# Attention outputs that leave the values transposed with weights applied before, and a last expert whose rows are added by a product

## The reference

```python
# layer 1, per head; p_c, p_s, p_w are softmax weights of the three branches
return gb[:, :, 0] * o_c + gb[:, :, 1] * o_s + gb[:, :, 2] * o_w
...
def expert_block(args):
    xblk, e = args
    hid = jax.nn.silu(xblk @ w_gate[e]) * (xblk @ w_up[e])
    return hid @ w_down[e]
...
y = jnp.zeros_like(xt).at[row_token].add(yb * row_weight[:, None].astype(yb.dtype))
```

## Time and profile before

| what | us |
|---|---|
| median of 3 runs | 1696.51 (1694.89 to 1697.32) |
| the profiled execution | 1696.19 |
| its span | 1694.4 |
| attention of layer 0 | 203 to 254 |
| experts of layer 0, first product to last | 330 to 802 |
| attention of layer 1 | 1001 to 1122 |
| experts of layer 1, first product to last | 1196 to 1670 |

### The profile page before, as it was taken

How to read it: one execution, slowest core, us unless ns; L and a number is a source line. 1 busy time by engine, 2 the same in 40 slices (tenths; PEclk the granted TensorE clock), 3 DMA queues, 4 the chain that set the end, 5 groups by cost and what they waited for, 6 DMA issues and landing times.

```text
span 1694.4 us, 20980 instructions
## 1 busy us (share of the span) xinstructions
PE 1589.3 (94%) x7948; PEld 753.0 (44%) x7948; DVE 434.3 (26%) x1112; ACT 393.7 (23%) x897; POOL 200.4 (12%) x297
## 2 busy tenths in 40 slices
PE   7999899799999999998799989999799999999993
PEld 4545574433333333332446457855333333333331
DVE  1585651610000000000321235643500000000002
ACT  2444451311111111111100136632211111111110
POOL 1241220000000000000101012320000000000000
PEclk9999999899999999999899989999799999999997
DMA  7120307379999999999924120042699999999996
GB/s 236 64 86 7 112 5 297 137 300 421 421 422 421 422 421 423 422 422 371 302 34 170 39 66 2 1 184 115 250 413 422 421 421 422 422 422 422 423 422 248
DMA packets 117162, 467.24 MB, mean 276 GB/s; under 512 B 40346, under 2 KB 46746, under 8 KB 68205
## 3 DMA queue, kind: packets, MB, share of 16 engines
q1 hardware_dynamic: 107724, 449.63, 66.1%
q10 hardware_dynamic: 4256, 8.40, 1.4%
q0 software_dynamic: 5120, 8.41, 1.3%
HBM read 455.88 MB, written 18.91 MB: 280 GB/s over the span
## 4 chain that ended last, share of the span: by engine, by line
PE 77%; SPq 11%; DMA 5%; DVE 3%; issue 2%; ACT 1%; POOL 1%; ACTq 0%; DVEq 0%; POOLq 0%
PE bank L1793 19%; PE bank L1806 10%; SPq L1741 9%; PE bank L1768 9%; PE bank L1432 8%; PE bank L558 7%; PE bank L811 6%; PE bank L446 4%; DMA arena<-in_moe_w_up 3%; PE bank L411 3%; PE bank L1783 2%; SPq L1750 2%; PE bank L892 2%; PE bank L428 2%; PE bank L1799 1%
## 5 line engine op out<-in xcount | busy, mean ns | idle before, releaser
L1793 PE MATMUL bank<-arena 128*64 128x512 f32 x2048 | 451.4, 592 | 8.1 <-DMA arena<-in_moe_w_up 6.7
L1793 PEld LDWEIGHTS bank<-arena 128*64 128x64 f32 x2048 | 143.5, 137 | 304.6 <-issue 294.0
L1806 PE MATMUL bank<-arena 128*64 128x512 f32 x1024 | 230.6, 592 | 2.2 <-DVE arena L1897 2.2
L1893 DVE TENSOR_TENSOR arena<-arena,bank 128x256 f32<-128x256 f32 x64 | 26.9, 421 | 644.4 <-ACT arena L1883 644.4
L1768 PE MATMUL bank<-arena 128*64 128x512 bf16 x1280 | 168.2, 395 | 9.7 <-DVE arena L1763 6.4
L1812 POOL DMA_INDIRECT y_d<-arena,slot_row x64 | 62.7, 979 | 904.7 <-ACT arena L1888 891.1
L1432 PE MATMUL bank<-arena 128*128 128x512 f32 x320 | 138.1, 593 | 0.8 <-ACT arena L328 0.8
L1806 PEld LDWEIGHTS bank<-arena 128*64 128x64 f32 x1024 | 72.2, 137 | 124.5 <-issue 111.2
L1883 ACT ACTIVATE arena<-bank 128x256 f32<-128x256 f32 x64 | 24.5, 383 | 408.2 <-PE bank L1793 408.2
L558 PE MATMUL bank<-arena 128*128 128x512 f32 x256 | 111.9, 594 | 0.0
L811 PE MATMUL bank<-arena 128*128 128x512 f32 (+1 forms) x288 | 105.3, 525 | 0.0
(11 more groups left out here) (287 smaller groups left out, 1434.8 us busy)
## 6 DMA issues: line engine op xcount, KB each, us to landing
arena<-in_moe_w_gate SPq DMA_DIRECT2D x128, 1024.0 KB, 20.1
arena<-in_moe_w_up SPq DMA_DIRECT2D x128, 1024.0 KB, 22.9
arena<-in_moe_w_down SPq DMA_DIRECT2D x62, 2048.0 KB, 23.2
arena<-in_even_w_in SPq DMA_DIRECT2D x4, 2048.0 KB, 7.9
arena<-y_d ACTq DMA_DIRECT2D x8, 1024.0 KB, 8.2
arena<-bias_row_d SPq DMA_DIRECT2D x2, 3584.0 KB, 11.6
arena<-in_odd_w_in SPq DMA_DIRECT2D x3, 2048.0 KB, 8.9
arena<-in_even_w_out SPq DMA_DIRECT2D x2, 2048.0 KB, 8.0
```

What stands on the lines that cost most here:

```text
L1793: mm = nc.tensor.matmul(bank[1][fh * CAP:(fh + 1) * CAP, :], xeT[:, j, half * CAP:(half + 1) * CAP], wgu[u][:, :, n, fh * FH:(fh + 1) * FH ...
L1806: mm = nc.tensor.matmul(bank[3][dh * CAP:(dh + 1) * CAP, :], hidT[:, j, fh * CAP:(fh + 1) * CAP], wd[u][:, n, dh * 512:(dh + 1) * 512], st ...
```

## The change

**Attention.** Units are put together into quads: four heads of one tile and one branch. Layer 1's quads come as selected, window, compressed for each group of four heads; layer 0's as heads 0 to 3 and 4 to 7. When the four exponentials are there, GpSimd makes the four weights (1/sum, with the gate in layer 1), and VectorE multiplies the exponentials by them before they are transposed, 1024 columns at a time at 512 keys, 768 at 384 and a whole quad from 256 down. Transposes stand six steps behind their unit, so values at least seven behind the quad's last one. In the values product the operands trade places: the values are loaded, the transposed weights of four heads are the moving operand (512 columns in layer 1, two products of 256 columns onto the two halves of the output partitions in layer 0). The output comes out transposed as the projection needs it; layer 1's three branches and all their key tiles are summed in one bank. ScalarE copies it once per four heads. `even_finish`, `odd_finish` and the twelve turns of attention output are gone; four turns of the Mamba half stay. The copies out of the transposes' banks alternate between ScalarE and VectorE. Eight slots hold exponentials instead of four. The first product of the projection is done before the last quad's transposes.

**Last expert.** Expert 31 isn't scattered. VectorE makes ones times weights for its slots (`last_ones`), TensorE transposes them (`last_T`), and two products per tile with the expert's 64 rows per half go into eight banks; VectorE adds them. Rows of the other 31 experts are fetched by SP as soon as expert 30 has been scattered, into weight slot 0, and are added with weights that are 0 where the expert is the last. Because rows of the last expert are never written, `y_d` is filled with zeros first, from a zeroed `z`, by two DMAs of 4 MB that ScalarE issues in the even mixer; `z` is written only when they are done. Two chunks of layer 1's projection weights are loaded behind the fetch instead of one ahead of it, and a third after the last products.

```diff
             def pe(self, pe, drain):
+                for t in range(self.steps):
+                    if t < len(self.units):
+                        u = self.units[t]
+                        if not (u.get("paired") and u["r"] % 2):
+                            self.scores(pe, [u, self.units[t + 1]] if u.get("paired") else [u])
+                    if t == len(self.units) + NT:
+                        drain()
+                    for g in self.turn_at[t]:
+                        self.turn(pe, g)
+                    for q, kt in self.value_at[t]:
+                        self.values(pe, q, kt)
...
+            TURN, SCALE = 6, 2
...
+                    L, last = q["L"], 4 * n + 3
...
+                    per = 4 if 4 * L <= DM else 2
+                    for k in range(4 // per):
+                        c["s"] += 1
+                        for u in q["units"][per * k:per * k + per]:
+                            u["scaled"] = c["s"]
+                        self.scale_at[last + self.SCALE + k].append(dict(quad=q, lo=per * k, n=per))
+                    q["scaled"] = c["s"]
+                    per, q["groups"] = NT // q["nk"], []
+                    for lo in range(0, 4, per):
...
+                        self.turn_at[4 * n + lo + per - 1 + self.TURN].append(g)
+                    for kt in range(q["nk"]):
+                        self.value_at[last + self.TURN + 1 + kt].append((q, kt))
+                    q["o"] = c["o"]
+                    if q["last"]:
+                        self.out_at[last + self.TURN + 1 + q["nk"]].append(q)
...
             def act(self, act):
+                for t in range(self.steps):
+                    for g in self.turn_at[t]:
+                        if g["copy"] == "act":
+                            self.copy_out(act, g)
+                    for q in self.out_at[t]:
+                        act.wait_ge(self.sem("pv"), q["m"] + 1)
+                        nc.scalar.activation(q["dst"], split(bank[4 + q["o"] % 2][:, :], 4, P), ACT.Copy).then_inc(self.sem("o"), 1)
...
             def dve(self, dve, link):
...
                         dve.wait_ge(self.sem("qk"), u["a"] + 1)
-                        if u["a"] - 4 >= self.base["a"]:
-                            dve.wait_ge(self.sem("tr"), self.by_a[u["a"] - 4]["n"] + 1)
+                        if t >= 8:
+                            dve.wait_ge(self.sem("tr"), self.units[t - 8]["group"]["n"] + 1)
...
+                    for op in self.scale_at[t]:
+                        q, lo, n = op["quad"], op["lo"], op["n"]
+                        slot = q["units"][lo]["a"] % 8
+                        p = self.p[:, slot:slot + n, 0:q["L"]]
+                        dve.wait_ge(self.sem("coef"), q["m"] + 1)
+                        nc.vector.tensor_tensor(p, p, att_coef[:, q["m"] % 4, lo:lo + n].unsqueeze(2).broadcast_to((P, n, q["L"])),
+                                                ALU.mult).then_inc(self.sem("sc"), 1)
+                    for g in self.turn_at[t]:
+                        if g["copy"] == "dve":
+                            self.copy_out(dve, g)
...
                 if c == 0:
+                    act.wait_ge(S("zeros"), past("zeros") + 1)
+                    for q in range(2):
+                        act.dma_start(y_d[q].rearrange("(p a r) c -> p a (r c)", p=P, a=4),
+                                      z.rearrange("p i c -> p (i c)").unsqueeze(1).broadcast_to((P, 4, NT * DI))).then_inc(S("y_zero"), 16)
...
+            act.wait_ge(S("y_zero"), past("y_zero") + 32)
             for i in range(NT):
                 n = J_Z + i
                 ev(n, z[:, i, :], bank[n % 4][:, :]).then_inc(S("ep_ev"), 1)
...
+            sp.wait_ge(S(f"{t}_gu"), L * NE + NE - 1)
+            fence(sp, t, L)
+            fetch(lambda i: f"{t}_yin{i}")
             if L == 0:
                 odd_early(sp)
...
+            pe.wait_ge(S("m_lT"), past("m_lT") + L + 1)
+            pe.wait_ge(S(f"{t}_y"), L * NE + NE + 1)
+            for i in range(NT):
+                for h in range(2):
+                    cs = slice(h * CAP, (h + 1) * CAP)
+                    mm = nc.tensor.matmul(bank[2 * i + h][:, :], last_T[cs, i * P:(i + 1) * P], yb[cs, (NE - 1) % RING, :],
+                                          start=True, stop=True)
+                mm.then_inc(S("m_fin"), 1)
...
+            add_fetched(0)
+            for i in range(1, NT):
+                add_fetched(i)
+                add_last(i - 1)
+            add_last(NT - 1)
```

More of the change, by code:

```diff
@@ L398, in done @@
             def done(self, eng):
-                self.finished(eng, len(self.order) - 1)
+                self.out(eng, self.after["o"] - 1)
             def mixed(self, eng, i):
-                for u in self.all:
-                    if "src" in u and u["tile"] == i:
-                        self.copied(eng, u)
+                for g in self.groups:
+                    if g.get("tile") == i:
+                        self.copied(eng, g)
+                self.out(eng, max(q["o"] for q in self.quads if q["tile"] == i))
             def scores(self, pe, us):
@@ L450, in pe @@
-            def pe(self, pe):
-                N = len(self.seq)
-                for t in range(N + 3):
-                    u = self.seq[t] if t < N else {}
-                    if "m" in u and not (u.get("paired") and u["b"] % 2):
-                        self.scores(pe, [u, self.seq[t + 1]] if u.get("paired") else [u])
-                    if 2 <= t < N + 2:
-                        self.turn(pe, self.seq[t - 2])
-                    if t >= 3 and "m" in self.seq[t - 3]:
-                        self.values(pe, self.seq[t - 3])
@@ L586, in route, with drain @@
                     mm.then_inc(S("m_rmm"), 1)
-            project(0, TILES[0])
-            att.tail_turns(pe)
-            for i in TILES[1:]:
+            def drain():
+                att.scored(pe, att.after["a"] - 1)
+                project(0, TILES[0])
+            att.pe(pe, drain)
+            project(0, TILES[1])
+            att.done(pe)
+            for i in TILES[2:]:
                 project(0, i)
@@ new lines, in products, with even_turn @@
+            def products(o, pT, kt):
+                return [(o[r * HD:(r + 1) * HD, half * 2 * P:(half + 1) * 2 * P], kvd[:, kt, O_V:O_V + HD], pT[:, r::2, :])
+                        for r in range(2)]
+            return dict(tile=i, L=L, units=units, products=products, first=half == 0, fresh=True, ends=True, last=half == 1,
+                        dst=mixT[:, 4:8, i * P:(i + 1) * P])
+        def even_turn(i):
+            return dict(tile=i, src=rows_m[:, 0, i, :], dst=mixT[:, 0:4, i * P:(i + 1) * P], ready=(S("ssm_row"), NT))
@@ L1350, in build @@
+        even_att = Attention([even_quad(i, half) for i in TILES for half in range(2)],
+                             {1 + i: even_turn(i) for i in range(NT)}, 2 * EW + 2 * KD * 512, O_XBCS, even_weigh)
         o0 = HEADS * TW
@@ L1689, in build @@
+        odd_att = Attention([odd_quad(i, g, b) for i in TILES for g in range(OG) for b in (SEL, WIN, CMP)],
+                            {}, O_OW + 2 * KD * 512, O_CT, odd_weigh, before=even_att)
         weight = sb("weight", [P, 2, NT])
@@ L2045, in body @@
                 down(pe, t, c, cu, u)
+                if after == 1:
+                    pe.wait_ge(S("m_lones"), past("m_lones") + L + 1)
+                    for i in range(NT):
+                        mm = nc.tensor.transpose(bank[7][:, i * P:(i + 1) * P], last_w[:, i].rearrange("p h s -> p (h s)"), ident[:])
+                    mm.then_inc(S("m_lturn"), 1)
             per_expert(pe, L, body)
```

367 lines of the change are left out of this document (187 added, 180 removed).

## The result

The changed kernel takes 1728.7 us, median of four runs (1722.3 to 1731.1), against 1696.9 (1694.9 to 1699.6) for the kernel before beside it: 1.018 times as long, 95% interval 1.0147 to 1.0214. I had forecast 1698.6 and a range up to 1708. The profiled execution is the shortest of the four, 1722.3, with a span of 1720.4, so 26.0 more than the span before.

| stretch | before | after | change |
|---|---|---|---|
| layer 0: first logits to projection | 48.0 | 45.3 | -2.7 |
| layer 0: projection and router | 76.2 | 77.9 | +1.7 |
| layer 0: copy of the last expert's y to the square of the next norm's tile 3 | 21.9 | 15.1 | -6.8 |
| layer 1: first logits to projection | 119.0 | 159.3 | +40.3 |
| layer 1: projection and router | 74.2 | 76.1 | +1.9 |

What follows compares the result with a forecast made beforehand. TensorE, busy 94% of the span, was taken as the bound, with latency chains after the last expert. 1696.2 - 6.3 - 7.3 - 3 + 19 = 1698.6 us; own range 1693 to 1704, with rivals 1685 to 1708.

Steps and rivals of the forecast that it cites:

- Tails: After the last expert in both layers: earlier fetch and last rows by products gain 6.3 and 7.3 us, together 13.6.
- Layer 0's attention: Output turns removed and values in two column halves: net -3 us, bounds -8 and +4.
- A gain of 8, as by the speedup alone: Layer 0's values by the skill's table, up to 2x at 64 columns: 8 us instead of 3, sum 1693.6.
- Layer 1's attention: TensorE waits for quads' weights and slots: 121.7 to about 140.5 us, net +19, bounds +8 and +24.
- rival B: Granted clock falls in layer 1's attention stalls, slow products follow: +8 us, 1706.6; chance 0.18.
- the clock leaves 1.00 there: Sign in layer 1's long tiles that the forecast is wrong in size; gaps above 5 us were the other.
- The other two quads' weights are covered: Layer 1's long tiles: besides window's weights and the slot reuse, the selected and compressed quads' weights cost no stall.
- stalls in the long tiles: Layer 1, per twelve units: about 3.3 us before window's transpose and 1.2 for slot reuse at 512 keys; similar at 384.
- Edits taken as nothing: Zeroing y_d, ScalarE's new wait, later MoE weight loads and GpSimd's last wait cost nothing; zeroing uncovered up to 2 us.
- A: Faster: in layer 1 only the window stall remains (+10), layer 0's column halves cost no drain (-6): 1686.6; chance 0.28.
- C: Tails' fetch ends no earlier: gain 7 instead of 13.6 us, 1705.2; chance 0.12 shared with D.
- D: Two halves of layer 0's values don't overlap: +4 us instead of -3, 1705.6; chance 0.12 shared with C.

Runs made afterwards that it cites:

- run 4: Changed kernel plus filler products where TensorE stands still in layer 1's attention, into a transposes' bank that is overwritten afterwards; 1717.9 us.
- run 3: Changed kernel with layer 1's weights made on VectorE just ahead of the quad's scaling, none on GpSimd; 1721.6 us.
- run 2: Changed kernel with one swap in VectorE's order: the copy of a transposed block stands ahead of the next quad's scaling; 1710.7 us.
- run 5: Changed kernel with copies ahead of scalings, and twelve slots instead of eight for layer 1's exponentials; 1705.7 us.
- run 6: Changed kernel with copies ahead of scalings, twelve slots, and layer 1's transposes eight steps behind their unit instead of six; 1691.0 us.
- run 1: Kernel before, with its old attention, given only the new ends of both layers and the zeroing of y_d; 1683.5 us, ratio 0.9914.

## Why the prediction was right or wrong, step by step

**Tails: right.** Forecast 6.3 and 7.3, in the profiles 6.8 and 7.4, alone on the chip 13.5 against 13.6. The intermediate steps held too: fetch issued at 793.7 (forecast 794.8), first additions at 799.7 (800.5), the last additions of tile 3 from 812.7 to 815.2 (816.7, in a run that was 1.0 earlier). By my own terms the sums come to 800.1 for the first landing and to gains of 6.4 and 7.5, a few tenths that change nothing.

**Layer 0's attention: right at its cut, a third of it in the whole layer.** Forecast -3, measured -2.7. But the end of the stage moved: the last quad's transposes and values now stand behind the projection's first product. From first logits to the experts' first product it is 124.2 before and 123.2 after, so 1.0 remains. The stage also varies with the clock: the same code took 45.3 in after, 45.6 in run 4 and 47.5 in run 3. And TensorE was 87% busy in it, not over 90% as I had said. The price of the change between half and full array holds in the timeline of after: values and transposes in turn start 0.58 and 0.59 apart.

```profile
220.75 0.65 PE L471 MATMUL bank<-arena 128*64 128x256 f32 x4
221.33 0.66 PE L456 MATMUL bank<-ident,arena 128*128 128x128 f32 x4
221.92 0.44 PE L471 MATMUL bank<-arena 128*64 128x256 f32 x2
```

One such pair, four value records and four transposes, takes 1.17. I had 0.78 + 0.44 = 1.22. A gain of 8, as by the speedup alone, did not come.

**Layer 1's attention: wrong by half, +19 forecast, +40 measured.** From first logits to projection that is 140.4 against 159.3. Of the 18.9 between them 14.4 are the clock, 3.6 idle time and 0.9 work. Another 2.7 is my starting point: I took 121.7 for the old attention, which from its first logits to the projection takes 119.0.

The step that failed first is the choice between the forecast and rival B. I had put the clock's fall at 18 in 100 and at 8 us, because the clock had stayed 1.00 at 83% busy in the last tile. But there the idle time came in pieces of 0.7 at most, here in pieces of up to 4.3, so that tile told little of this stage. The recorded sign "the clock leaves 1.00 there" came true: the term was wrong in size, and what was left out of it is the clock's 14.4. The size of a piece doesn't decide alone either, as the last section shows. Run 4 moves the clock's cost while the waits stay, and the time follows; run 2 moves both.

The step that failed second is "The other two quads' weights are covered". I had asked who needs the scaling's result, and found the transposes. I had not asked what stands behind the scaling in VectorE's own queue: the copy of the quad before it, behind that this quad's values, and behind the values on TensorE the last scores of the quad after next. So the weights and values of neighbouring quads were strung into one chain. The copies alternate between ScalarE and VectorE, and at 128 keys TensorE's idle time before the values is 2.0, 2.4 and 3.0 where VectorE copies and 0.6 to 1.3 where ScalarE does. At 256 keys my idle time was 6.8 against 10.2, and with the swap it is 7.2. At 128 keys my 10.4 looks right beside 11.1, but for a wrong reason: I had a round over the weights that ends at the transposes, the idle time lies before the values, and a third of it left with one swap. In the profiles the swap takes 11.4 off the attention, 6.1 idle time, 4.9 clock and 0.4 work. The rest of the 18 by the medians lies in executions without a trace; their granted clocks, below, point to the clock again.

What I had worked out as stalls in the long tiles was right: 9.0 and 8.8 against 8.9 and 8.4, the large piece 3.45 against 3.3, the small one 1.0 against 1.2, and in runs 5 and 6 they went away for the most part. At 512 keys the sum agrees partly by luck: it holds 2.14 before the very first transposes, which I had not listed, and in the first round window's piece was only 2.32.

**Edits taken as nothing.** The zeroing: right, by run 1. That the first product hides the last quad's transposes and values: only their latency. They moved behind it with their work, and the projection is 1.9 longer, which I had not counted. The 1.7 more in layer 0's projection I had not forecast at all. In run 1, with the old attention, it is the clock: 0.84 in the first 11 us of the projection, where it was 1.00 before. In after it is the last quad's work and 0.8 of idle time before its values.

**The rivals.** A (only the window stall remains, column halves cost nothing) is refuted by the second stall that run 5 took away and by the pairs of 1.17. C and D are refuted by run 1 and by layer 0's 45.3. B was true, and under-sized: I had let half of 12 stalls be followed by two slow microseconds, and after has some 29 us at the lower clock. With 13.4 in place of 8 it would have given 1712. The rest up to the profiled 1722.3 is mostly idle time and work in the attention, 4.5, the projections' 3.6 and the 2.7 of my starting point; the median of the kernel lies another 6.4 above its profiled execution.

## What to carry to other kernels

When a step with a long wait is put into an engine's queue, list not only who needs its result but each instruction that stands behind it there, and who needs that; here a copy that feeds TensorE belonged ahead of a scaling that waits for another engine. Where a change brings longer idle pieces into a stage than any it had, give the clock a term of its own: here it was 13.4 us, beside 33.7 of added idle time. When latencies are made longer, lengthen the pipeline by as many steps in the same edit: eight steps and twelve slots took 20 us off, where a faster weights computation gave 7, and nothing once the latency was covered. And a stage that keeps its engine 98% busy leaves little to win by rearranging: the best new order of layer 1 still stood at 123.3 against 119.0, so here the part worth keeping was the tails, and with them perhaps layer 0.

## What the runs showed of the hardware

Idle pieces inside a busy stage were often paid twice: behind one of 2.14 and one of 4.30 us TensorE worked at 1.2 GHz for some three and five microseconds (1002.6 to 1006, 1099.9 to 1105). But not each time: in the 384-key tile of after the clock stayed at 1.00 through idle pieces of 2.38 and 3.19, so the length of one piece does not decide alone, and the same tile with nearly the same waits had 0.92 in run 2. Shorter pieces came before a fall too: behind 1.31, 0.90 and 0.68 the clock of after is at 1.2 GHz from 1118.7 to 1122.1 (the last two lines). The runs of the changed kernel are spread over 8.8 us, those of before over 4.7. The mean granted clocks of its four executions are 0.976, 0.971, 0.969 and 0.969, in the order of their times 1722.3, 1726.4, 1730.9 and 1731.1; that the spread comes from the clock is likely by this, though only the first has a trace.

```profile
1056.00:1060.00 4.00, 1.56 (x8) 0.87 (x8) 2.41 (x5) 1.33 (x7) 1.19 (x2) 1.00 0.01 2
1060.00:1064.00 4.00, 4.00 (x20) 2.42 (x19) 1.37 (x6) 1.50 (x5) 1.47 (x3) 1.00 0.00 0
1076.00:1080.00 4.00, 0.81 (x8) 0.73 (x7) 1.86 (x7) 2.09 (x10) 1.47 (x3) 1.00 0.00 0
1080.00:1084.00 4.00, 4.00 (x19) 2.44 (x18) 1.97 (x7) 1.39 (x5) 1.47 (x3) 1.00 0.00 0
...
1110.00:1118.60 8.60, 5.72 (x33) 3.96 (x32) 5.08 (x19) 4.58 (x16) 2.90 (x6) 1.00 0.00 0
1118.60:1122.10 3.50, 3.50 (x12) 2.47 (x12) 1.13 (x4) 0.81 (x5) 1.47 (x3) 0.51 0.02 5
```

In run 1 the mean clock was 0.84 over 11 us in which TensorE was busy without a gap, with 1.2 GHz from 257.0 to 260.4. What brings that about stays open.
